# A two-block transformer kernel: the feed-forward up projection by Strassen's seven block products, and the down projection as a stage of its own

## What is computed

```python
D_FF = 2816                          # 22 tiles of 128 channels each for gate and value
h2 = rms_norm(x, norm2_g[l])
up = h2 @ w_up[l]                    # [1024, 1024] @ [1024, 5632]
up = causal_depthwise_conv(up, ffn_dw_w[l])      # width 3, per channel
gate, val = jnp.split(up, 2, axis=-1)
x = x + (jax.nn.silu(gate) * val) @ w_down[l]    # [1024, 2816] @ [2816, 1024]
```

## Time and profile before

| | us |
|---|---|
| median of 3 runs | 2760.18 (2756.51 to 2762.19) |
| profiled execution, its own time | 2755.93 |
| its span in the trace | 2754.3 |
| TensorE busy | 2702.6 |
| VectorE busy | 1627.7 |
| ScalarE busy | 716.9 |
| GpSimd busy | 327.4 |
| moved by DMA over the span | 287.66 MB |

### The profile page before, as it was taken

One profiled execution on the slowest core, in us unless ns is written; L12 is line 12 of the kernel. 1 busy time (PEld: TensorE's weight loads), 2 busy tenths in 40 slices (PEclk: granted clock), 3 DMA queues, 4 the chain that ended last, 5 costly groups with the idle time before them and its releaser, 6 DMA issues.

```text
span 2754.3 us, 35646 instructions
## 1 busy us (share of the span) xinstructions
PE 2702.6 (98%) x13436; PEld 2186.4 (79%) x13452; DVE 1627.7 (59%) x2058; ACT 716.9 (26%) x1319; POOL 327.4 (12%) x310
## 2 busy tenths in 40 slices
PE   9999989999999999999999999999999999999987
PEld 7767758888888888878888888888887888888766
DVE  8956563764555455575454454454466666666665
ACT  5333341411111111132021021021034444444441
POOL 0899800000000000021000000000000000000000
PEclk9999999999999999999999999999999999999999
DMA  5211113253434343424222222222233222222214
GB/s 192 78 62 59 61 47 122 99 207 122 152 122 153 136 157 134 166 77 168 92 76 76 91 76 76 91 76 76 91 143 133 77 76 76 76 77 79 73 70 160
DMA packets 50891, 287.66 MB, mean 104 GB/s; under 512 B 6800, under 2 KB 7952, under 8 KB 20880
## 3 DMA queue, kind: packets, MB, share of 16 engines
q1 hardware_dynamic: 23072, 119.92, 12.5%
q0 software_dynamic: 14544, 105.91, 11.2%
q10 hardware_dynamic: 13216, 61.02, 5.8%
HBM read 249.08 MB, written 29.36 MB: 101 GB/s over the span
## 4 chain that ended last, share of the span: by engine, by line
PE 91%; DVE 3%; ACT 1%; issue 1%; DVEq 0%; ACTq 0%
PE OBB L243 11%; PE OBB L245 11%; PE OBB L244 11%; PE PB L243 10%; PE PB L245 10%; PE PB L244 10%; PE TBB L1000 4%; PE TBB L243 3%; PE TBB L245 3%; PE TBB L244 3%; PE PB L1049 2%; PE OBB L1114 2%; PE PB L1055 1%; PE OBB L1109 1%; PE PB L2216 1%; PE PB L2218 1%
## 5 line engine op out<-in xcount | busy, mean ns | idle before, releaser
L243 PE MATMUL PB<-HH,WH 128*128 128x512 f32 x1296 | 513.6, 396 | 2.2 <-DVE HL L405 1.2
L245 PE MATMUL PB<-HH,WL 128*128 128x512 f32 x1296 | 504.7, 389 | 0.0
L244 PE MATMUL PB<-HL,WH 128*128 128x512 f32 x1296 | 504.4, 389 | 0.0
L243 PE MATMUL OBB<-HH,WH 128*128 128x512 f32 x1120 | 453.7, 405 | 3.0 <-issue 3.0
L245 PE MATMUL OBB<-HH,WL 128*128 128x512 f32 x1120 | 438.5, 391 | 0.0
L244 PE MATMUL OBB<-HL,WH 128*128 128x512 f32 x1120 | 438.3, 391 | 0.0
L243 PEld LDWEIGHTS PB<-HH,WH 128*128 128x128 f32 x1296 | 243.3, 188 | 58.4 <-issue 5.1
L244 PEld LDWEIGHTS PB<-HL,WH 128*128 128x128 f32 x1296 | 243.4, 188 | 54.6 <-issue 4.8
L245 PEld LDWEIGHTS PB<-HH,WL 128*128 128x128 f32 x1296 | 243.3, 188 | 51.2
L259 DVE TENSOR_TENSOR WL<-RAW,WH 128x2048 fp32r<-128x2048 f32 x101 | 237.5, 2352 | 53.5 <-DMA WH<-units 51.8
L2762 POOL DMA_DIRECT2D WH<-units x85 | 46.0, 541 | 1811.9 <-PE PB L243 891.9
(11 more groups left out here) (394 smaller groups left out, 4168.7 us busy)
## 6 DMA issues: line engine op xcount, KB each, us to landing
WH<-units POOLq DMA_DIRECT2D x85, 1024.0 KB, 5.1
RAW<-units SPq DMA_DIRECT2D x85, 1024.0 KB, 4.7
gs<-units ACTq DMA_DIRECT2D x16, 1024.0 KB, 4.8
gu<-gs ACTq DMA_DIRECT2D x16, 1024.0 KB, 3.9
RAW<-gu SPq DMA_DIRECT2D x16, 1024.0 KB, 4.9
WH<-gu POOLq DMA_DIRECT2D x16, 1024.0 KB, 5.5
tmpd<-xr SPq DMA_DIRECT2D x112, 64.0 KB, 2.0
A<-xT SPq DMA_DIRECT2D x8, 512.0 KB, 8.5
```

The costliest lines, as they stand in the source:

```text
L243: first = pe.e.matmul(out, wh, xh, start=start, stop=False)
L244: pe.e.matmul(out, wh, xl, start=False, stop=False)
L245: return pe.e.matmul(out, wl, xh, start=False, stop=stop), first
```

## The change

Tiles 0 and 1 are made as before, in the new `up_first_*` functions, but both from the unscaled tokens. The other 20 tiles are made by Strassen's scheme over 2x2 blocks: the weights of a tile (gate, value) by (first, last 512 input channels), and the normed tokens (first, last 512 channels) by (first, last 512 tokens). Seven products M0 to M6 of 4 blocks x 3 = 12 matmuls each take the place of eight: 84 matmuls a tile. Each product needs its own weight piece (five of the seven are sums or differences of two quarters, made by GpSimd, then split by ScalarE and VectorE) and its own token piece `XH`, `XL` (five are sums or differences, made once). VectorE combines the products in PSUM (`combined`). The results of the up part go to DRAM (`ub`), since the token pieces fill the memory. The normed tokens overwrite `A`, which was stored to DRAM (`xf`) and is read back at the start of the down stage.

The down stage runs by token halves and output tiles in the order `DOWN_SEQ`: 22 units of 16 blocks, 48 matmuls each (before: 11 units of 96), 352 x 3 = 1056 matmuls as before. Each result tile is read from DRAM in halves (44 reads of 256 KiB), split by ScalarE and VectorE. All 16 rounds of the gain work stand in this stage, one for each of its first 16 units, with three buffers.

```diff
-FF_GROUPS = FF_TILES // 2
-FF_LOOPS = (FF_GROUPS - 1) // 2
-U_RET = U_FFN + 3 * FF_GROUPS
+U_DOWN = U_FFN + 2
+DOWN_SEQ = ([(h, m, k) for h, b in ((0, 0), (0, 1), (1, 0)) for k in range(FF_TILES) for m in range(4 * b, 4 * b + 4)]
+            + [(1, m, k) for m in (4, 5, 6) for k in range(FF_TILES)]
+            + [(1, 7, k) for n in range(KT) for k in (6 + n, 14 + n)] + [(1, 7, k) for k in range(6)])
+DOWN_UNITS = len(DOWN_SEQ) // 16
+U_RET = U_DOWN + DOWN_UNITS
...
+        def up_pe(pe, ph):
+            def product(p, j, n, i):
+                if j:
+                    pe.e.wait_ge(dve_done, at_mark(pe, "dve", f"w{p}_0", i))
+                else:
+                    pe.e.wait_ge(dve_done, at_prev(pe, "dve", f"w{p}_1", i))
+                    if ph == UP_PHASES[0]:
+                        pe.e.wait_ge(dve_done, done_in("dve", "ffn_first", f"x{p}"))
...
+            def body(i):
+                for j in range(2):
+                    pe.e.wait_ge(dve_done, at_prev(pe, "dve", f"cg_{j}", i))
+                    product(0, j, 0, i)
+                    product(1, j, 1, i)
+                    product(2, j, 2, i)
+                    product(3, j, 3, i)
+                    pe.e.wait_ge(act_done, at_mark(pe, "act", f"m2_{j}", i))
+                    product(4, j, 0, i)
+                    pe.e.wait_ge(dve_done, at_mark(pe, "dve", f"q_{j}", i))
+                    product(5, j, 1, i)
+                    pe.e.wait_ge(dve_done, at_mark(pe, "dve", f"r_{j}", i))
+                    product(6, j, 2, i)
...
+        def up_first_act(act):
...
+            for p in range(3):
+                mix_high(act, p)
+            gate_value(0)
+            for p in range(4):
+                e.wait_ge(summed, FIRST_SUMS[f"p{p}"])
+                piece_high(act, p, 1, 2)
+            silu(0)
+            for p in (3, 4, 5):
+                mix_high(act, p)
+            e.wait_ge(pe_done, at_mark(act, "pe", "v1"))
+            for p in (4, 5):
+                piece_high(act, p, 1, 2)
+            gate_value(1)
+            mix_high(act, 6)
+            e.wait_ge(summed, FIRST_SUMS["p6"])
+            piece_high(act, 6, 1, 2)
+            silu(1)
...
+        def up_pool(pool):
...
+            pool.wait_ge(dve_done, done_in("dve", "ffn_first", "t7"))
+            mixed(2)
+            pool.wait_ge(raw_up[0], 16)
+            pool.wait_ge(pe_done, done_in("pe", "ffn_first", "v0"))
+            for p in range(4):
+                piece_sum(pool, p, 2)
+            for p, name in ((3, "h1"), (4, "h3"), (5, "h5"), (6, "v1")):
+                pool.wait_ge(pe_done, done_in("pe", "ffn_first", name))
+                mixed(p)
+            piece_sum(pool, 6, 2)
+            for t in range(3, FF_TILES):
+                pool.wait_ge(raw_up[t % 2], 16 * (t // 2))
+                for p in (0, 1, 2, 3, 6):
+                    pool.wait_ge(pe_done, up_at("pe", t - 1, f"M{p}_{(t - 1) % 2}"))
+                    piece_sum(pool, p, t)
...
+        def down_act(act):
...
+            for k in range(4, 8):
+                tile_high(act, 0, k)
+            e.wait_ge(dve_done, up_at("dve", FF_TILES - 1, "mu_1"))
+            for n in range(2):
+                e.wait_ge(u_out[n], 16 * (FF_TILES // 2))
+            e.dma_start(A[:, :, :], io["xf"].rearrange("(k p) s -> p k s", p=P)).then_inc(x_back, 16)
+            for k in range(8, FF_TILES):
+                tile_high(act, 0, k)
+            gain_load(act, 0)
+            gain_load(act, 1)
+            for r in range(2 * DIFF_HEADS):
+                if 6 <= r < 12:
+                    for k in range(4 * (r - 6), min(4 * (r - 6) + 4, FF_TILES)):
+                        tile_high(act, 1, k)
+                gain_store(act, r)
+                if r + 2 < 2 * DIFF_HEADS:
+                    gain_load(act, r + 2)
...
+        def down_dve(dve):
...
+            for k in range(4, 8):
+                tile_low(dve, 0, k)
+            for u in range(DOWN_UNITS):
+                low_part(dve, U_DOWN + 1 + u)
+                if u < 2:
+                    for k in range(8 + 7 * u, 15 + 7 * u):
+                        tile_low(dve, 0, k)
+                if u < 2 * DIFF_HEADS:
+                    if 6 <= u < 12:
+                        for k in range(4 * (u - 6), min(4 * (u - 6) + 4, FF_TILES)):
+                            tile_low(dve, 1, k)
+                    gain_unit(dve, u)
...
+        def ffn_sp(sp, plain):
...
+                store(t, V[:, j, :], up_at("dve", t, f"mu_{j}"))
+                if t == FF_TILES - 2:
+                    for k in range(8):
+                        tile(0, k)
+            for u in range(DOWN_UNITS - 1):
+                plain(U_DOWN + 1 + u, 0)
+                if u < 2:
+                    for k in range(8 + 7 * u, 15 + 7 * u):
+                        tile(0, k)
...
+            run(12, U_DOWN)
+            up_pool(pool)
+            pool.wait_ge(pe_done, up_at("pe", FF_TILES - 1, "M3_1"))
+            high(U_DOWN, 0, io["units"][U_DOWN:U_DOWN + 1])
+            run(U_DOWN + 1, U_RET)
...
+            for k in range(1, KT - 1):
+                add_square(k)
+            high(U_RET, 0, io["units"][U_RET:U_RET + 1])
```

More of the change, by code:

```diff
@@ L1843, in att_dve @@
             conv_out_dve(dve)
-        G = work("G", [P, 2, S], F32, 0)
-        V = work("V", [P, 2, S], F32, 8 * K)
-        UH = [work(f"UH{n}", [P, 2, S], F32R, (16 + 16 * n) * K) for n in range(2)]
-        UL = [work(f"UL{n}", [P, 2, S], F32R, (24 + 16 * n) * K) for n in range(2)]
-        FF_OUT = [TBB, OBB]
-        def up_bank(b, j, i):
-            return FF_OUT[b] if i is None and j else PB[b]
-        def ffn_units(steps):
-            at_u, offs = 0, []
-            for what, _ in steps:
-                offs.append(at_u)
-                at_u += 2 if what == "up" else 1
-            return offs
@@ L1866, in ffn_banks @@
[L1866 to L1882 removed]
+        RAW1 = at("RAW1", [P, UNIT], F32, 104 * K)
@@ L1884, in first_total, with in_phase @@
+        def in_phase(x, ph, body):
+            x.start(ph, "ffn_first")
+            x.tiles_of = None
+            if ph == UP_PHASES[1]:
+                x.iters = UP_LOOPS
+                with x.e.Fori(0, UP_LOOPS) as i:
+                    body(i)
+            else:
+                body(None)
         def first_total(pe):
@@ new lines, in down_at @@
+        def down_at(part, k):
+            off = W0 + (16 + 4 * k) * K if k < 6 else (32 + 4 * (k - 6)) * K
+            return at(f"U{part}{k}", [P, HALF], F32R, off + (0 if part == "H" else 2 * K))
+        UDH = [down_at("H", k) for k in range(FF_TILES)]
+        UDL = [down_at("L", k) for k in range(FF_TILES)]
+        us_in = [work(f"us_in{n}", [P, HALF], F32, (40 + 2 * n) * K) for n in range(8)]
+        gs = [work("gs0", [P, UNIT], F32, 0), work("gs1", [P, UNIT], F32, 8 * K), at("gs2", [P, UNIT], F32, 104 * K)]
@@ new lines, in tile_low, with down_pe @@
+        def tile_low(dve, h, k):
+            dve.e.wait_ge(act_done, tile_mark("act", "uh", h, k))
+            dve.e.tensor_tensor(UDL[k][:, :], us_in[(h * FF_TILES + k) % 8][:, :], UDH[k][:, :].bitcast(F32),
+                                ALU.subtract).then_inc(dve_done, dve.mark(f"ul{h}_{k}"))
+        def down_pe(pe):
+            pe.start("ffn_last", "ffn_up_last")
+            pe.tiles_of = None
+            seen = set()
+            for n, (h, m, k) in enumerate(DOWN_SEQ):
+                if n % 16 == 0:
+                    slot = unit(pe, U_DOWN + n // 16)
+                if (h, k) not in seen:
+                    pe.e.wait_ge(dve_done, tile_mark("dve", "ul", h, k))
+                    seen.add((h, k))
+                first_k = k == 0 if (h, m) != (1, 7) else k == 6
+                last_k = k == FF_TILES - 1 if (h, m) != (1, 7) else k == 5
+                if first_k and h == 0 and m < 4:
+                    pe.e.wait_ge(dve_done, up_at("dve", FF_TILES - 2, "cg_0"))
+                elif first_k and h == 0:
+                    pe.e.wait_ge(dve_done, up_at("dve", FF_TILES - 1, "cg_1"))
+                elif first_k:
+                    pe.e.wait_ge(dve_done, at_mark(pe, "dve", f"y0_{m}"))
+                c = n % 16 * P
+                mm, first = mm3(pe, DOWN_BANKS[m], WH[slot][:, c:c + P], WL[slot][:, c:c + P],
+                                UDH[k][:, :], UDL[k][:, :], first_k, last_k)
+                if pe.fresh:
+                    first.then_inc(unit_begun, 1)
+                    pe.fresh = False
+                if last_k:
+                    mm.then_inc(pe_done, pe.mark(f"d{h}_{m}"))
+                if h == 0 and m == 7 and not last_k:
+                    mm.then_inc(pe_done, pe.mark(f"k{k}"))
+                if (h, m) == (1, 7) and k >= 14:
+                    mm.then_inc(pe_done, pe.mark(f"e{k - 14}"))
```

653 lines of the change are left out of this document (398 added, 255 removed).

## The result

| | before | changed |
|---|---|---|
| median of 4 runs, run in turn on one chip | 2758.35 us (2756.43 to 2762.19) | 2828.99 us (2824.88 to 2832.67) |
| profiled execution / its span | 2755.93 / 2754.3 us | 2824.88 / 2823.2 us |
| ratio, 95% interval | | 1.0257 (1.0243 to 1.0272) |

What follows compares the result with a forecast made beforehand. TensorE, busy 98% of the span, was taken to bound the kernel. Gain -54.7, start +22, turn +26, down rounds +33, end +4 and clock +6 sum to +36: forecast 2794 us, range 2762 to 2828.

Steps and rivals of the forecast that it cites:

- The gain, -54.7: Up stage, tiles 2 to 21: 12 matmuls fewer each, 240 in all at 0.228 us, saving 54.7 us.
- the up stage, 0: Up stage in steady state: VectorE, ScalarE and GpSimd fit within TensorE's 19.2 us a tile, so no loss.
- Rival 2: Up stage: VectorE becomes the bound at 22.3 us a tile against 19.2, adding 62 us, total 2856; chance 0.08.
- rival 3: Up stage: each of 140 products begins with a 0.2 us pause, 28 us more, total 2822; chance 0.04.
- The start, +22: First Strassen tile: VectorE and GpSimd's token sums take turns on a shared port, 22 us lost; bounds 7 and 30.
- The turn, +26: Up to down stage: WH late 2, RAW behind a store 6, low part behind first gain product 18; bounds 9, 35.
- The down rounds, +33: Down stage's first 16 rounds: 4 MiB each at 410 GB/s leaves no slack, 33 us lost; bounds 0 and +50.
- (a): Seven down rounds: WH landing, low part and hand-over make 11.8 us against 10.9 of matmuls, 6 us lost in all.
- (b): Down rounds with four second-half half tiles: 5 MiB and more VectorE work make 16 us each, 18 us lost.
- Clock, +6: Longer TensorE pauses, open at the start and the turn, lower the granted clock for a time, 6 us lost.
- a share well under 1: Down rounds: sign of a wrong forecast, which expected a DMA share near 1 for some 150 us.
- Rival 1: Transfers and port do not bind: at 480 GB/s or more 2739, with rarer port turns 2724; chance 0.12.

Runs made afterwards that it cites:

- no_sums: Changed kernel without the five token sums at the start, token pieces 2 to 6 made from one quarter: 2812.20 us, ratio 1.0185.
- dve_sums: Changed kernel with the five token sums at the start moved from GpSimd to VectorE: 2819.71 us, ratio 1.0217.
- raw_first: Changed kernel with SyncE asking RAW ahead of tile 21's store and of four half-tile reads in four later rounds: 2810.95 us, ratio 1.0183.
- double_load: spread2 with WH loaded from DRAM again and gain pairs issued behind the next WH's landing: 2768.95 us, ratio 1.0038.
- spread2: Changed kernel with WH copied by ScalarE, RAW asked earlier, token sums on VectorE, gain work later, half-tile reads and A's reload spread: 2725.27 us, ratio 0.9881.

## Why the prediction was right or wrong, step by step

- **The gain, -54.7, and the up stage, 0: right.** 1491 matmuls in 340.00 us without idle are 0.228 each. Rival 2 (VectorE the bound) and rival 3 (0.2 ahead of each product) are out: VectorE was busy 291.6 of 340, or 16.4 of a tile's 19.2 (said 15.3). That VectorE's work on PSUM isn't held by GpSimd's sum was read from a row of the kernel before, in the middle of the sum from 1215.05 to 1218.47:

```profile
1216.14 1.21 DVE L2032 TENSOR_TENSOR A<-A,TBB 128x1024 f32<-128x1024 f32 x1
```

- **The start, +22: right in its mechanism, 4 too high.** The waits were 18.2; the low clock behind them (0.59 in 560 to 580) was a term of its own. Each part met a sum as counted: the four `WL` parts were said to end at 560.6 and ended at 559.6. no_sums confirms the cause; dve_sums confirms it by its sign only.
- **The turn, +26: right.** First unit 3.4 (said 2), second 3.3 (6), third 18.8 (18): 25.5. The order that was said for the third is in the trace: the load of `gs` is issued at 1000.93 behind the copies and lands within 5 us, VectorE waits for it, and the low part comes only then.

```profile
1000.93 0.84 ACTq L2421 DMA_DIRECT2D gs<-units  x2
...
1005.75 2.36 DVE L2431 TENSOR_TENSOR gs<-gs,par 128x1024 f32<-128x1024 f32 x2 [13.48 <-DMA gs<-units]
1008.03 2.28 DVE L268 TENSOR_TENSOR WL<-RAW,WH 128x2048 fp32r<-128x2048 f32 x1
```

- **The down rounds, +33: wrong, by 30 us of the 33 that the sum is short.** Bounds were 0 and 50; it was 62.9. The term was made of three. (a) "it lands some 9.2 us on, 2.28 for the low part and the hand-over make 11.8: 0.9 lost in seven rounds, 6". In place of 11.8 there were 13.6 to 14.9 in all but one of nine such rounds, 24.8 lost. `WH` is asked 1.1 to 1.4 after a unit's begin (0.3 were counted for both hand-overs), and lands 10.0 later (median from 1060 to 1240). (b) Half-tile rounds, "16", 18 lost: they took 20.0, 17.3, 17.0 and 14.9, 25.4 lost. The step saw bytes and VectorE's time there, not that SyncE asks `RAW` behind reads that wait for VectorE; with that order changed, raw_first was 18.0 us faster, and in its trace these four rounds 10.5 shorter. (c) The first two, 9: 12.5. The error behind all three is one: what a round loses was taken from a volume at 410 GB/s, and the upper bound from a slower rate, 370 GB/s. Only the plain rounds were written as a chain, and there the landing came from the rate. A rate bounds nothing where the next request is issued only after the last has arrived; the engines then stand partly idle, at 300 GB/s. The chain begin, ask, land, low part, begin should have been the sum, and its slowest landing the bound. (The 83 MB of the step count all 44 half-tile reads, of which eight are asked before the stage, at 947.5; that makes 81 MB and doesn't change the sum.)
- **The end, +4: right,** 4 as what the other terms leave. **Clock, +6: half its size.** The pauses and the lower level of the clock are there, but cost 8.2 at the start and 4.9 at the turn, 13 in all. In the rounds a slow unit ate its own wait, as said. With 4 too much at the start, 30 too little in the rounds and 7 too little here the sum of +36 becomes the 69 of the traces.
- **What would show it:** "a share well under 1" in the rounds was named as a sign of being wrong, and it was there (0.82). Rival 1 took it for the case in which the rounds cost nothing. Here it was instead the mark of a chain: a low share beside an idle TensorE.
- By the limit of about 358 GB/s which the Trainium skill gives (page "DMA: Bandwidth & Descriptors", section "Specifications"), 20 us more were noted, which would have come nearer by chance. The trace still disagrees: 393 GB/s over 40 us in double_load, 375 in spread2.

## What to carry to other kernels

When work per unit is halved, don't ask only if the bytes of a round fit at the full rate; write down the chain from one begin to the next, with each request at the time when its buffer comes free and the landing time beside everything issued with it. A DMA share of 0.8 beside an idle TensorE is a reason to look for a chain or an order. Here it was cured by fewer dependent requests (a copy on an idle engine instead of a second load), by the place of a request in its queue, and by spreading what isn't urgent. A gain of 55 us in matmuls was lost, and 34 of it won, in such places: 2829 and 2725 have the same matmuls.
